# Delta scans whose first triangular blocks are made in the stage before, and which make the first input halves of the stage behind

## What is computed

```python
kb = k * beta
vb = v * beta
a_mat = jnp.where(strict, jnp.einsum('bhnid,bhnjd->bhnij', kb, k) * decay, 0.0)
eye = jnp.eye(C, dtype=jnp.float32)
t_mat = lax.linalg.triangular_solve(eye + a_mat, jnp.broadcast_to(eye, a_mat.shape),
                                    left_side=True, lower=True, unit_diagonal=True)
u = jnp.einsum('bhnij,bhnjd->bhnid', t_mat, vb)
w = jnp.einsum('bhnij,bhnjd->bhnid', t_mat, kb * jnp.exp(gc)[..., None])
qk = jnp.where(tri, jnp.einsum('bhnid,bhnjd->bhnij', q, k) * decay, 0.0)
...
def step(s, inp):
    u_i, w_i, qk_i, qd_i, kd_i, gl_i = inp
    v_new = u_i - jnp.einsum('bhcd,bhde->bhce', w_i, s)
    o_i = jnp.einsum('bhcd,bhde->bhce', qd_i, s) + jnp.einsum('bhcj,bhje->bhce', qk_i, v_new)
    s = s * gl_i[..., None, None] + jnp.einsum('bhcd,bhce->bhde', kd_i, v_new)
    return s, o_i
```

## Time and profile before

| | us |
|---|---|
| median of 3 runs (2605.36 to 2612.03) | 2608.62 |
| the profiled execution's own time | 2609.77 |
| its span, first to last instruction | 2608.0 |
| scan of group 0, first to last instruction | 1266.8 to 1432.6 |
| scan of group 1 | 1536.8 to 1699.0 |

### The profile page before, as it was taken

How to read it: one execution, slowest core, us unless ns; L and a number is a source line. 1 busy time by engine, 2 the same in 40 slices (tenths; PEclk the granted TensorE clock), 3 DMA queues, 4 the chain that set the end, 5 groups by cost and what they waited for, 6 DMA issues and landing times. The chain is left out here.

```text
span 2608.0 us, 45966 instructions
## 1 busy us (share of the span) xinstructions
PE 2504.1 (96%) x18822; PEld 2105.0 (81%) x18822; DVE 1631.6 (63%) x2459; ACT 793.6 (30%) x1371; POOL 1213.2 (47%) x966
## 2 busy tenths in 40 slices
PE   8999999999899999999898989999899999999998
PEld 6878888888578888878788878877898888788887
DVE  7869849751568939757665566546787236771551
ACT  4224314231534403333544254423563100210000
POOL 3555554556545455533542254322543455454553
PEclk9999999999999999999999999999999999999999
DMA  4233334322024333321101211111212322222222
GB/s 167 81 129 123 135 138 145 102 105 97 17 81 161 132 142 138 115 73 66 42 31 34 80 35 35 35 47 52 57 20 75 104 93 86 82 97 100 94 99 78
DMA packets 51176, 229.63 MB, mean 88 GB/s; under 512 B 5280, under 2 KB 12464, under 8 KB 32432
## 3 DMA queue, kind: packets, MB, share of 16 engines
q1 hardware_dynamic: 50992, 226.99, 25.3%
HBM read 224.80 MB, written 2.17 MB: 87 GB/s over the span
## 5 line engine op out<-in xcount | busy, mean ns | idle before, releaser
L246 POOL TENSOR_TENSOR ring_rounded<-ring,ring_rounded 128x512 fp32r<-128x512 f32 (+2 forms) x711 | 952.0, 1369 | 1009.8 <-DVE ring_rounded L237 720.4
L300 PE MATMUL psum<-arena_rounded,ring_rounded 128*128 128x512 f32 (+1 forms) x2820 | 1092.4, 387 | 32.8 <-DVE arena_rounded L651 10.1
L301 PE MATMUL psum<-arena_rounded,ring_rounded 128*128 128x512 f32 (+1 forms) x2820 | 1082.7, 384 | 0.0
L302 PE MATMUL psum<-arena_rounded,ring_rounded 128*128 128x512 f32 (+1 forms) x2820 | 1082.4, 384 | 0.0
L300 PEld LDWEIGHTS psum<-arena_rounded,ring_rounded 128*128 128x128 f32 x2820 | 531.0, 188 | 146.6 <-issue 22.1
L302 PEld LDWEIGHTS psum<-arena_rounded,ring_rounded 128*128 128x128 f32 x2820 | 531.0, 188 | 106.0
L301 PEld LDWEIGHTS psum<-arena_rounded,ring_rounded 128*128 128x128 f32 x2820 | 531.5, 188 | 102.8 <-issue 1.2
L237 DVE CAST ring_rounded<-ring 128x2048 fp32r<-128x2048 f32 (+5 forms) x134 | 145.6, 1087 | 477.8 <-PE psum L302 460.4
L849 ACT ACTIVATE arena<-psum,vectors 128x512 f32<-128x512 f32 x88 | 68.0, 772 | 258.1 <-DVE psum L889 258.1
L262 ACT ACTIVATE ring_rounded<-ring 128x2048 fp32r<-128x2048 f32 (+1 forms) x57 | 104.6, 1835 | 100.1 <-PE psum L302 65.5
L2268 DVE SCALAR_TENSOR_TENSOR arena<-psum,vectors,arena 128x510 f32<-128x510 f32 (+3 forms) x160 | 96.0, 638 | 12.2 <-ACT arena L2194 9.6
(11 more groups left out here) (462 smaller groups left out, 3244.6 us busy)
## 6 DMA issues: line engine op xcount, KB each, us to landing
ring<-in_w_up SPq DMA_DIRECT2D x44, 1024.0 KB, 4.9
arena<-in_w_mod SPq DMA_DIRECT2D x48, 512.0 KB, 5.5
ring<-in_w_down SPq DMA_DIRECT2D x32, 704.0 KB, 4.1
ring<-in_w_mup SPq DMA_DIRECT2D x16, 1024.0 KB, 4.9
ring<-in_w_mdown SPq DMA_DIRECT2D x16, 1024.0 KB, 4.8
ring<-in_w_gdn SPq DMA_DIRECT2D x12, 1024.0 KB, 4.8
ring<-in_w_lru_in SPq DMA_DIRECT2D x10, 1024.0 KB, 4.9
ring<-in_w_odd_in SPq DMA_DIRECT2D x10, 1024.0 KB, 4.8
```

Source lines behind the costliest of these rows:

```text
L246: last = pool.tensor_tensor(self.rounded(low), raw, self.rounded(high).bitcast(F32), ALU.subtract)
L300: pe.matmul(out, r(wh), r(xh), start=start, stop=False)
L301: pe.matmul(out, r(wh), r(xl), start=False, stop=False)
L302: return pe.matmul(out, r(wl), r(xh), start=False, stop=stop)
```

## The change

The triangles, masks and eye of each scan's first tile are made by VectorE in the tail of the input stage (`dve_triangle`), in a place of memory whose old contents TensorE has read by then (`scan_places`). In exchange the last query tile's four taps and SiLU go to the start of the scan (`dve_query_taps`); the scan's 16 dummies go. The first tile's query sums, turn, means and roots each move one level later, its grams go to level 4 (d = 0) and level 2 (d = 1), the first two query spreads go around the far products, and the scaling of the last two queries stands together. The split of the unit that the next stage needs first moves from the input stage to GpSimd's third tile of the scan. The first two of the next stage's eight input tiles are rounded by ScalarE and subtracted by GpSimd at the end of the scan, so the next stage handles six. PSUM banks of direction 0 change their roles to suit.

```diff
 def scan_bank(d, role):
-    return 4 * d + (role if d else (role + 2) % 4)
+    return 4 + role if d else (2, 0, 3, 1)[role]
+
+
+def first_gram_bank(d):
+
+    return scan_bank(1, MB) if d else scan_bank(0, ZB)
+
+
+def scan_places(d):
+
+    at = [512 * i for i in range(12 * d, 12 * d + 12)]
+    for early, late in ((0, 3), (1, 8), (2, 5)):
+        at[early], at[late] = at[late], at[early]
+    return at
...
+    def dve_triangle(self, dve, d):
+        m, c, e, z = self.m, self.m.vchain, self.e[d], self.z1[d]
+        wide = lambda x: x.rearrange("p (a b) -> p a b", a=1).broadcast_to([x.shape[0], GH, x.shape[1]])
+        dve.wait_ge(m.sem("kscaled"), m.count("kscaled", 2))
+        dve.wait_ge(m.sem("firstgram"), m.count("firstgram", d + 1))
+        dve.wait_ge(m.sem("firstexp"), m.count("firstexp", d + 1))
+        for h in range(GH):
+            last = dve.scalar_tensor_tensor(e[:, h, :], self.gram(d)[:, h, :],
+                                            scan_gcol(m, self.group, BETA, SCAN_TILES[d][0], d, h), e[:, h, :],
+                                            ALU.mult, ALU.mult)
+        last.then_inc(c.up(), 1)
+        dve.wait_ge(c.sem, c.now())
+        for i in range(2):
+            r, to = slice(HB * i, HB * i + HB), slice(HB * (i ^ d), HB * (i ^ d) + HB)
+            last = dve.tensor_tensor(z[to], e[r, :, r], wide(m.lev[r, 1 - d, 0, :]), ALU.mult)
+        last.then_inc(c.up(), 1)
+        dve.wait_ge(c.sem, c.now())
+        dve.tensor_tensor(z, z, wide(m.eye[:, :]), ALU.add).then_inc(m.up("firstz"), 1)
+
+    def dve_query_taps(self, dve, v):
+        m, c, o, out = self.m, self.m.vchain, self.qt[:, GH - 1, :], self.m.psum[:, scan_bank(0, MB), :]
+        for i in (0, 1, 3, 4):
+            s = i - 2
+            a, b = max(0, -s), T - max(0, s)
+            ins = dve.scalar_tensor_tensor(o[:, a:b], out[:, a + s:b + s],
+                                           col(v["conv_qkv"], i * 24 + GH * self.group + GH - 1), o[:, a:b],
+                                           ALU.mult, ALU.add)
+            if i == 4:
+                ins.then_inc(m.up("qtaps"), 1)
+            else:
+                ins.then_inc(c.up(), 1)
+                dve.wait_ge(c.sem, c.now())
...
+XN_HELD = 2
+
+
+def round_xn(m, act, xh, ks=range(XN_HELD, KD)):
     xn = m.at(XN_AT, KD, TA)
-    for k in range(KD):
+    for k in ks:
         act.activation(m.rounded(xh[:, k, :]), xn[:, k, :], ACT.Copy).then_inc(m.up("xhigh"), 1)
 def split_xn(m, dve, xh, xl):
...
         step.act_decay(act, 1)
         tap(us[5], 1)
         silu(us[5], 0)
-        silu(us[5], 1)
...
         taps_of(us[5], 0)
-        begin(us[5])
-        taps_of(us[5], 1)
+        m.dve_unit(dve, us[5])
+        step.dve_triangle(dve, 0)
+        step.dve_triangle(dve, 1)
...
-        for unit in us[4:]:
-            m.pool_unit(pool, unit)
+        m.scan_lo = us[4]
+        m.pool_unit(pool, us[5])
...
         def beside(t, k, d):
-            if (t, k) in ((0, 5), (1, 1)):
-                query_spread(2 * t + d)
+            if (t, k) == (1, 1):
+                query_spread(2 + d)
             if k == 1 and t >= 2:
                 state_product(t - 1, d)
             if k == 2 and 2 <= t + 1 < NA:
                 query_gram(t + 1, d)
-            if k == 3 and t + 1 < NA:
+            if k == FIRST_GRAMS[d] if t == 0 else k == 3 and t + 1 < NA:
...
-        m.hold(pe, 16, scan_bank(0, YB))
         seed_left(0)
         seed_right(0)
         for t in range(NA):
             for k in range(1, LEVELS + 1):
                 left(t, k)
-                if (t, k) == (0, 1):
+                if (t, k) == (0, 2):
                     query_sums()
-                if (t, k) == (0, 2):
+                if (t, k) == (0, 3):
                     query_turn()
                 beside(t, k, 0)
...
+            if t == 0:
+                query_spread(0)
             if t - 1 >= 2:
                 output(t - 1, 0)
             if t + 1 < NA:
                 seed_right(t + 1)
             far_right(t)
+            if t == 0:
+                query_spread(1)
...
-        for h in range(GH):
+        def query_square(h):
             act.activation(qsq[h], qt[:, h, :], ACT.Square).then_inc(m.up("qsquare"), 1)
+
+        query_square(0)
         x_copy(0, 0, 0)
         x_copy(0, 0, 1)
+        query_square(1)
+        query_square(2)
+        act.wait_ge(m.sem("qtaps"), m.count("qtaps", 1))
+        act.activation(qt[:, GH - 1, :], qt[:, GH - 1, :], ACT.Silu).then_inc(m.up("qsilu"), 1)
+        act.wait_ge(m.sem("qsilu"), m.count("qsilu", 1))
+        query_square(GH - 1)
...
+        round_xn(m, act, xh, range(XN_HELD))
...
+        def next_low(k):
+            pool.wait_ge(m.sem("xhigh"), m.count("xhigh", k + 1))
+            pool.tensor_tensor(m.rounded(xl[:, k, :]), xn[:, k, :], m.rounded(xh[:, k, :]).bitcast(F32),
+                               ALU.subtract).then_inc(m.up("xlow"), 1)
...
-        first_level(0, 0)
-        first_level(0, 1)
...
+            if t == 2:
+                m.pool_unit(pool, m.scan_lo)
             if t == 3:
                 m.pool_kept(pool)
+        next_low(0)
         query(LAST, 0)
         query(LAST, 1)
+        next_low(1)
...
-        for d in range(2):
-            dve.memset(B[d]["ZF"][half[1 - d], :, half[d]], 0.0).then_inc(m.up("zfzero"), 1)
-        triangle(0, 0)
-        triangle(0, 1)
+        step.dve_query_taps(dve, v)
+
         def beside(t, k, d):
-            if (t, k) in ((0, 5), (1, 1)):
-                query_scaled(2 * t + d)
+            if (t, k, d) == (1, 1, 0):
+                query_scaled(2)
+                query_scaled(3)
...
+                query_scaled(0)
+                query_scaled(1)
```

More of the change, by code:

```diff
@@ L1850, in __init__, with gram @@
         self.e = TokenTiles(m, group).decays
-        self.kt = m.at(KT_AT, GH, TA)
+        self.kt, self.qt = m.at(KT_AT, GH, TA), m.at(QT_AT, GH, T)
+        self.z1 = [m.at(scan_places(d)[8], GH, HB) for d in range(2)]
+    def gram(self, d):
+        return self.m.psum[:, first_gram_bank(d), :].rearrange("p (h c) -> p h c", c=P)
     def pe_gram(self, pe, d):
@@ L1855, in pe_gram @@
         k = slice(n * P, (n + 1) * P)
-        out = self.m.psum[:, scan_bank(d, MB), :].rearrange("p (h c) -> p h c", c=P)
+        out = self.gram(d)
         for h in range(GH):
@@ L1878, in split_xn @@
     xn = m.at(XN_AT, KD, TA)
-    for k in range(KD):
+    for k in range(XN_HELD, KD):
         hi, lo = m.rounded(xh[:, k, :]), m.rounded(xl[:, k, :])
-        dve.wait_ge(m.sem("xhigh"), m.count("xhigh", k + 1))
+        dve.wait_ge(m.sem("xhigh"), m.count("xhigh", k + 1 - XN_HELD))
         dve.tensor_tensor(lo, xn[:, k, :], hi.bitcast(F32), ALU.subtract).then_inc(m.up("xready"), 1)
@@ L2427, in gdn_scan_stage @@
     LAST = NA - 1
+    FIRST_GRAMS = (4, 2)
     bank = lambda d, i: m.psum[:, scan_bank(d, i), :].rearrange("p (h c) -> p h c", c=P)
@@ L2913, in dve @@
                 if (t, k) == (0, 1):
+                    for d in range(2):
+                        dve.memset(B[d]["ZF"][half[1 - d], :, half[d]], 0.0).then_inc(m.up("zfzero"), 1)
+                if (t, k) == (0, 2):
                     query_rows()
-                if (t, k) == (0, 2):
+                if (t, k) == (0, 3):
                     query_means()
-                if (t, k) == (0, 4):
+                if (t, k) == (0, 5):
                     query_roots()
```

45 lines of the change are left out of this document (22 added, 23 removed).

## The result

| | before | after |
|---|---|---|
| median, us | 2609.5 (6 runs, 2601.0 to 2612.0) | 2590.3 (6 runs, 2587.6 to 2592.0) |
| the profiled execution's own time | 2609.8 | 2592.0 |
| its span | 2608.0 | 2590.2 |

The ratio is 0.993, with a 95% interval of 0.9918 to 0.9942: faster by 0.6 to 0.8%. The forecast was 2590.8.

What follows compares the result with a forecast made beforehand. TensorE, busy 96% of the span, was taken as the bound, so only its idle or filler stretches count. Seams 6.0 + 6.1, tiles 2 x 0.85 and halves 2 x 2.0 give 17.8 us less: 2590.8, range 2586 to 2596.

Steps and rivals of the forecast that it cites:

- The seams into the scans: Input stage to delta scan: triangles and eye made earlier, dummies gone; seed 6.0 (group 0) and 6.1 us (group 1) sooner.
- the sum: Whole kernel: 6.0 + 6.1 + 2 x 0.85 + 2 x 2.0 = 17.8 us less, median 2590.8.
- The weight split put off: Four GpSimd operations (5.00 us) move from the input stage's tail into 7.99 us of GpSimd idleness in the scan; cost nothing.
- The first tile and the query chain: Scan's first tile to tile 2's third left product: taps' delay earned back, 0.85 us less in each group.
- S: The moment a scan's first real TensorE product, the seed, starts; later marks are given in us after it.
- The stop without a releaser: TensorE's 1.76 us stop in group 0's scan, nothing to wait for; one such stop kept in two scans, no gain.
- The halves: Next stage's first two input tiles prepared at scan end, so its first product comes at once: 2.0 us less per stage.
- The slower rival: Scan heads: without the 3.81 us of dummies the clock falls to 1.2 GHz, 13 more per scan, 2616.8; chance 0.02.

## Why the prediction was right, point by point

**The seams into the scans: right, and for the reasons given.** 6.0 and 6.1 were expected, 6.11 and 6.11 came. The eye on VectorE takes 0.42, the value taken; VectorE closes the stage in group 0 (1265.45 + 0.42 = 1265.87), the dummies in group 1 (1523.34). What the sum did not see is a condition of it: the 0.85 for two masks does not hold while GpSimd subtracts in SBUF. The row for it came from a scan in which GpSimd stood still.

**The weight split put off: "nothing" was the wrong step.** Its own removal costs nothing where it went, as said. But the working took it for an edit without value, and the run with it put back shows that without it the seams would have been 2.8 and 2.5 longer. The value was hidden in the masks' price. The sum came out right because it priced the two edits together.

**The first tile and the query chain: right in group 0, mark by mark, and less in group 1.** In group 0 the mask comes at S + 3.02 (3.2 expected), the third left product at 9.67 (10.0), the far product at 19.73 (19.9), the second tile's first left product at 24.93 with the 0.62 stop, so 24.31 (24.25), its third at 33.00, so 32.38 (32.4). In group 1 that third product stands at 33.86, 35.35 and 32.94 in the three profiles of the changed kernel; without the stops ahead of it, 32.90 to 32.96: 0.3 earned where 0.85 was expected.

**The stop without a releaser: the mechanism was right, the size was not.** The prediction let the stop move with the stream and kept one, at no gain. The kernel before had six such waits, of 3.7 us in all, and the sum looked only at the one of 1.76. A large one moved from group 0 to group 1, as allowed for; but the changed kernel has three to five, of 4.4 to 6.3 us in all. In the first profile the scans together gave 0.23 where 1.7 was expected; in the other two they took 2.8 and 0.8 more than before. Had the trace of before been counted in blocks of 256, the stop would have had its rule before the run: it lies where a block begins, and so do four of the five smaller ones in the same scan that were not priced. The page cited for it (the Trainium skill, Runtime: NRT & Kernel Launch, section "Instruction fetch mechanics") has the block and its 256 instructions as the traces show them; "mostly hidden" holds for most of the some 30 blocks of a scan, and fails where the fetch begins late.

**The halves: right.** 2.0 expected in each of two stages, 1.96 and 1.95 came, and 3.00 stood there again without them. Nothing of the last tile was lost to the subtractions (13.27 with them, 13.28 without).

**That the total hit to 0.5 us is partly luck.** The scans' missing 1.5 was made up by 1.47 behind the last seam, which no edit touches and which varies by more than that among the profiles. Over its 16 runs the changed kernel's median is 2591.2.

**The slower rival** ("the dummies were needed") is wrong in its price: where the clock did fall at the head of the scan, in the run without any dummies, the loss was 1.0 and 0.9, not 13. The first tile waits for VectorE and ScalarE so much that half clock on TensorE costs little there, and the clock did not stay down for the whole tile: it was back at 1.00 from S + 8.84 on. Half clock over a whole first tile was seen in no run.

## What to carry to other kernels

Where one engine runs many short instructions, number them in the trace before pricing an edit that adds or removes some: stops that share a remainder on division by the block's length belong to the instruction stream, and an edit anywhere ahead moves them. A filler that looks useless may be holding the stream in a good place, so test its removal together with a shift that puts the stream back. And price an operation from a row in which the neighbouring engine does what it will do behind the change.

## What was not expected of the hardware

- Where a row transfer is under way, the fetch of TensorE's next 256 instructions starts when its last packet ends (within 0.01 us, 7 of 7 profiles with the large stop), 5.0 to 5.6 us behind the block's start, and TensorE goes on 2.2 to 2.4 us after the fetch has begun. That the transfer is the cause is read from the traces and tested by no run.
- A 32-bit product with 128x128 weights takes nearly as long for 64 columns as for 128 (7.70 / 68 = 0.113 a pass against 4.18 / 36 = 0.116). On a quarter of the array a 64x64 pass takes 0.064 (2.42 / 38), in turn on all four quarters 0.021 (0.80 / 38).
- Two of VectorE's masks with both operands in SBUF take 2.83 instead of 0.85 while GpSimd subtracts, and GpSimd's four subtractions 5.34 instead of 5.00.
- After 4.5 us without work on TensorE the granted clock is 0.57 for the next 8.84 us; after 1.68 it stays at 1.00 in some scans and falls in others. What tells these apart is open, and so are the stops in group 0 (0.62, 0.78, 1.39 at the same product), whose fetch begins late with no transfer near.
